# The order of expert weight loads and of TensorE's up steps in a hybrid decoder layer

## The reference

```python
logits = tok @ w_router + b_router
top_val, top_idx = lax.top_k(logits, 4)
top_w = softmax(top_val)
# for each expert e, on the rows of tokens that chose it:
hgu = tok[rows] @ w_gu[e] + b_gu[e]               # 1024 -> 2048
gate = minimum(hgu[:, 0::2], 7.0)
up = clip(hgu[:, 1::2], -7.0, 7.0)
act = (up + 1.0) * (gate * sigmoid(1.702 * gate))
y = act @ w_down[e] + b_down[e]                    # 1024 -> 1024
out = out.at[rows].add(y * wts)
```

## Time and profile before

| | |
|---|---|
| median of 3 runs | 1312.96 us (1312.86 to 1314.96) |
| profiled execution, its time | 1314.96 us |
| profiled execution, its span | 1313.1 us |
| TensorE busy | 86% of the span |
| TensorE granted clock, mean | 0.919 |
| moved by DMA | 455.49 MB, mean 347 GB/s |

### The profile page before, as it was taken

How to read it: one execution, slowest core, us unless ns; L and a number is a source line. 1 busy time by engine, 2 the same in 40 slices (tenths; PEclk the granted TensorE clock), 3 DMA queues, 4 the chain that set the end, 5 groups by cost and what they waited for, 6 DMA issues and landing times.

```text
span 1313.1 us, 19225 instructions
## 1 busy us (share of the span) xinstructions
PE 1127.0 (86%) x7477; PEld 535.2 (41%) x7478; DVE 270.2 (21%) x732; ACT 217.7 (17%) x486; POOL 17.9 (1%) x25
## 2 busy tenths in 40 slices
PE   8999999999989987659966966799697969799857
PEld 4564767888543333123322321233222323233311
DVE  3234424463141111001100100011101101111100
ACT  2115422353021101001100100111010101011101
POOL 1100101000000000000000000000000000000000
PEclk9999999999979999779987977899888979899978
DMA  9942337334559999999999999979999999999995
GB/s 338 344 140 94 113 136 263 130 132 184 201 207 422 425 426 426 426 427 426 423 426 425 428 426 427 426 301 422 424 426 427 422 426 425 427 426 427 426 427 223
DMA packets 66599, 455.49 MB, mean 347 GB/s; under 512 B 7524, under 2 KB 13384, under 8 KB 33800
## 3 DMA queue, kind: packets, MB, share of 16 engines
q1 hardware_dynamic: 66008, 454.20, 84.2%
q10 hardware_dynamic: 448, 0.60, 0.1%
q0 software_dynamic: 112, 0.26, 0.1%
HBM read 454.00 MB, written 1.05 MB: 347 GB/s over the span
## 4 chain that ended last, share of the span: by engine, by line
PE 64%; DMA 24%; SPq 8%; issue 2%; DVE 1%; ACT 1%; ACTq 0%; DVEq 0%
DMA mq<-in_b_gu 24%; PE bank L1060 17%; PE bank L1085 10%; PE bank L590 6%; PE bank L730 6%; SPq L394 4%; SPq L505 4%; PE bank L1020 4%; PE bank L1028 3%; PE bank L1039 3%; PE bank L639 2%; PE bank L926 2%; PE bank L892 2%; PE bank L579 1%; PE bank L616 1%
## 5 line engine op out<-in xcount | busy, mean ns | idle before, releaser
L1060 PE MATMUL bank<-mem 128*32 128x512 f32 x2944 | 360.4, 633 | 157.2 <-DMA mq<-in_b_gu 157.2
L1060 PEld LDWEIGHTS bank<-mem 128*32 128x32 f32 x2944 | 93.5, 114 | 369.5 <-issue 367.2
L1085 PE MATMUL bank<-mem 128*32 128x512 f32 x1472 | 177.1, 624 | 1.1 <-ACT mem L1376 1.1
L1821 DVE TENSOR_SCALAR mem<-bank 128x256 f32<-128x256 f32 x46 | 19.5, 425 | 748.8 <-PE bank L1060 748.8
L1382 ACT ACTIVATE mq<-bank 64x512 f32<-64x512 f32 x46 | 27.1, 590 | 468.9 <-PE bank L1085 468.9
L1085 PEld LDWEIGHTS bank<-mem 128*32 128x32 f32 x1472 | 44.7, 114 | 134.4 <-issue 133.7
L1020 PEld LDWEIGHTS bank<-mem,sc 128*128 128x128 f32 x736 | 85.6, 195 | 18.8 <-issue 18.8
L1020 PE MATMUL bank<-mem,sc 128*128 128x64 f32 x736 | 88.8, 280 | 0.3 <-DVE mem L1797 0.3
L1028 PE MATMUL bank<-mq,mem 128*128 128x512 f32 x184 | 85.1, 605 | 1.5 <-ACT mem L1399 1.5
L590 PE MATMUL bank<-mem 128*128 128x512 f32 x192 | 83.2, 592 | 0.0
L730 PE MATMUL bank<-mem 128*128 128x256 f32 x320 | 71.3, 381 | 0.0
(11 more groups left out here) (296 smaller groups left out, 787.6 us busy)
## 6 DMA issues: line engine op xcount, KB each, us to landing
mem<-in_w_gu SPq DMA_DIRECT2D x128, 2048.0 KB, 32.7
mem<-in_w_down SPq DMA_DIRECT2D x64, 2048.0 KB, 37.1
mem<-in_w_in SPq DMA_DIRECT2D x13, 2048.0 KB, 10.5
mem<-in_w_out SPq DMA_DIRECT2D x2, 2048.0 KB, 8.3
mem<-in_w_mem_kv SPq DMA_DIRECT2D x2, 1024.0 KB, 7.0
mem<-in_w_mem_kv SPq DMA_DIRECT2D x1, 2048.0 KB, 9.5
mem<-in_cmp_w_k SPq DMA_DIRECT2D x1, 2048.0 KB, 8.5
mem<-in_cmp_w_v SPq DMA_DIRECT2D x1, 2048.0 KB, 8.3
```

Of the source, the lines that this page charges most:

```text
L1060: mm = nc.tensor.matmul(BH[n][32 * s:32 * s + 32, :], xgT[:, k, 32 * n:32 * n + 32], w[:, c, 512 * s:512 * s + 512], start=k == 0, stop=k ...
L1085: mm = nc.tensor.matmul(BG[64 * hh + 32 * two:64 * hh + 32 * two + 32, :], actT[:, o:o + 32], w[:, 2 * c + two, 512 * hh:512 * hh + 512], ...
```

## The change

SyncE's list gets another order. In a round, the bias rows of seat n+1 come first, then its chunks 0 and 1, then chunks 4 and 5 (`w_down`) of seat **n** (`here`, into the slots that the last item `g` of seat n-2 leaves), then chunks 2 and 3 of seat n+1. A last round loads only `w_down` of seat 31. On TensorE, up1 moves ahead of `down` of the item before, behind up0 and bias, and `turn` moves between bias and up1.

```diff
--- before.py
+++ after.py
@@ -492,31 +492,40 @@
             sp.wait_ge(S("x2_ready"), 2)
             load_chunk(sp, 1, 4, True)
 
-            def load_round(n, odd, first=False):
-
-                f = sp.value_load(idx[0:1, bass.ds(n, 1)], min_val=0, max_val=ITEMS - 1)
-                ahead = sp.value_load(idx[0:1, bass.ds(n + (AT_ORDER + 1), 1)], min_val=0, max_val=NE - 1)
-                for q in range(4):
-                    sp.wait_ge(S("gu_done"), f * 4 + (q + 1))
-                    load_chunk(sp, ahead, q, not odd)
-                    if q == 1:
-                        sp.wait_ge(S("brow_used"), f + 1)
-                        for m in range(4):
-                            sp.dma_start(brow[not odd][32 * m:32 * m + 1, :],
-                                         b_gu[bass.ds(ahead, 1), 512 * m:512 * m + 512]).then_inc(brow_in[not odd], 16)
-                    if q == 1 and first:
-                        sp.wait_ge(S("bdn_done"), 1)
-                        load_chunk(sp, 1, 5, True)
-                for q in (4, 5):
-                    sp.wait_ge(S("down_done"), f * 2 + (q - 3))
-                    load_chunk(sp, ahead, q, not odd)
+            def load_round(n, odd, ups=True, downs=(4, 5)):
+
+                if ups:
+                    f = sp.value_load(idx[0:1, bass.ds(n, 1)], min_val=0, max_val=ITEMS - 1)
+                    ahead = sp.value_load(idx[0:1, bass.ds(n + (AT_ORDER + 1), 1)], min_val=0, max_val=NE - 1)
+                    sp.wait_ge(S("brow_used"), f + 1)
+                    for m in range(4):
+                        sp.dma_start(brow[not odd][32 * m:32 * m + 1, :],
+                                     b_gu[bass.ds(ahead, 1), 512 * m:512 * m + 512]).then_inc(brow_in[not odd], 16)
+                    for q in (0, 1):
+                        sp.wait_ge(S("gu_done"), f * 4 + (q + 1))
+                        load_chunk(sp, ahead, q, not odd)
+                if len(downs) == 2:
+                    here = sp.value_load(idx[0:1, bass.ds(n + AT_ORDER, 1)], min_val=0, max_val=NE - 1)
+                    g = sp.value_load(idx[0:1, bass.ds(n - 1, 1)], min_val=0, max_val=ITEMS - 1)
+                    for q in downs:
+                        sp.wait_ge(S("down_done"), g * 2 + (q - 3))
+                        load_chunk(sp, here, q, odd)
+                else:
+
+                    sp.wait_ge(S("bdn_done"), 1)
+                    load_chunk(sp, 1, 5, True)
+                if ups:
+                    for q in (2, 3):
+                        sp.wait_ge(S("gu_done"), f * 4 + (q + 1))
+                        load_chunk(sp, ahead, q, not odd)
 
             sp.wait_ge(S("idx_ready"), 1)
-            load_round(1, True, first=True)
+            load_round(1, True, downs=(5,))
             with sp.Fori(1, NE // 2 - 1) as r:
                 load_round(r * 2, False)
                 load_round(r * 2 + 1, True)
             load_round(NE - 2, False)
+            load_round(NE - 1, True, ups=False)
             for t in range(NT):
                 sp.wait_ge(S("out_left"), t + 1)
                 sp.dma_start(out_t[:, t, 0:512], x2[:, t, 0:512]).then_inc(S("out_done"), 16)
@@ -1105,22 +1114,25 @@
                 def left_early(odd):
                     up(0, left, 0, odd)
                     bias(0, odd)
+                    if not first:
+                        turn(i - 1, 1, j - 1)
+                    up(1, left, 0, odd)
 
                 def left_late(odd):
-                    for q in range(1, 4):
-                        up(q, left, 0, odd)
+                    up(2, left, 0, odd)
+                    up(3, left, 0, odd)
 
                 def right_early(odd):
                     up(0, right, 1, odd)
                     bias(1, odd)
+                    turn(i, 0, j)
+                    up(1, right, 1, odd)
 
                 def right_late(odd):
-                    for q in range(1, 4):
-                        up(q, right, 1, odd)
+                    up(2, right, 1, odd)
+                    up(3, right, 1, odd)
 
                 pe.wait_ge(S("g_evac"), j * 2 + 1)
-                if not first:
-                    turn(i - 1, 1, j - 1)
                 either(left, left_early)
                 pe.wait_ge(S("g_evac"), j * 2 + 2)
                 if not first:
@@ -1136,7 +1148,6 @@
                     pe.wait_ge(S("y_evac"), j * 2)
                     pe.wait_ge(S("st_evac"), j)
                     scatter()
-                turn(i, 0, j)
                 either(right, right_early)
                 pe.wait_ge(S("a_evac"), i + 1)
                 either(left, lambda odd: down(left, odd))
```

## The result

The changed kernel took 1341.45 us (median of 4 runs, 1340.57 to 1343.23) against 1313.76 us before in the same comparison; the ratio is 1.0222, 95% interval 1.0204 to 1.0240. It is slower, by 27.7 us. The prediction was 1333.6, with a range of 1322 to 1344: the time lies in the range, 7.9 us above the forecast. The profiled execution took 1341.32 us with a span of 1339.5, so the spans differ by 26.4 us and the forecast for that difference was 20.6.

The account below looks back on a forecast made before the run. The stream of weights was taken to pace the expert part. Start 2.6, seat 1 3.2, seat 8 7.1, seat 16 12.8 and end -5.1 sum to 20.6: span 1333.7, forecast 1333.6 us, range 1322 to 1344.

Parts of the forecast that it names:

- the end: Behind the last chunk: gu3(31) lands third from last, so the last seat finishes sooner; -5.1 us, bounds -7.3 and -0.8.
- seat 1: Near 421 us: stream runs dry at 420.3 waiting for item 2's bias, resumes 423.5; +3.2 us, bounds 2.3 and 3.9.
- stop at seat 8: New hole at a three-item seat: gu0 waits for the third item's bias; 7.1 us, bounds 5.1 and 9.1.
- stop at seat 16: Four-item seat: hole of 22.7 us in place of 9.9; +12.8 us, bounds 10.8 and 14.8.
- Depth of the queue: SyncE's list: dn(s+1) stands behind the wait for seat s's last item, leaving 6 chunks, 29.9 us, instead of 8, 39.9.
- Rivals A: Faster, 1298 us: bias rows and gu0 no longer wait for gu1, the hole at 871 closes; chance 0.06.
- B: Same, 1313.7 us: holes as before, start lost, tail won; chance 0.05.
- C: Slower, less, 1323.7 us: only two missing chunks at seat 16 count, seat 8 stays closed; chance 0.10.
- The 2.0 us for the clock: Added to the holes at seats 8 and 16: down behind short waits runs slower, 5.34 us instead of 3.64.
- Rival D: Slower, more, 1341.9 us: clock stays at 1.2 GHz beyond each wait, both holes at bound, slow scatter; chance 0.12.
- The restart: After a stop of the stream: 1.5 us from issue to flow; with the skill's 0.6 us, 2.7 less, estimate 1330.9.
- Order on TensorE: Same matmuls, nothing to win inside a busy stretch; with no stream to hide under, only turn's place counts, 0.7 us.

Follow-up runs that it names:

- one-item kernel: Kernel before with every expert cut to one item, tokens beyond the first 32 left out: 1310.69 us, before 1314.09.
- the two other edits: Changed kernel with w_down of seat n first and bias rows between chunks 0 and 1; with one transfer for the rows 1305.44 us, before 1313.01.

## Why the prediction was right, and where it was not

The stops, which are the mechanism, came as forecast. The total did not: of the 5.8 us by which the spans' difference was missed, 5.5 are one term, the end. It and seat 1 lie outside their own bounds, and that the sum up to the end of the bulk fits to 0.3 us is in part luck, as errors of -1.5, +0.7 and +1.6 cancel in part.

| term | forecast | measured | from |
|---|---|---|---|
| start | +2.6 | +2.5 | stream flows from 395.3 (157 GB/s in 394:396) against 392.8 |
| stop at seat 1 | +3.2 | +1.7 | window 420:430 |
| stop at seat 8 | +7.1 | +7.8 | windows 620:640 |
| stop at seat 16 | +12.8 | +14.4 | 24.3 against 9.9 |
| end of the bulk | +25.7 | +26.0 | 1321.0 (221 GB/s in 1320:1322) against 1295.0 |
| behind the bulk | -5.1 | +0.4 | 18.5 against 18.1 |
| span | +20.6 | +26.4 | |

**Depth of the queue: right.** The stops came where they were forecast and nowhere else, and moving two issues takes them away. Rivals A, B and C fall with the 24.3 us at seat 16 and the new stop at seat 8. The chain inside the stop is exact: from dn(16)'s second half at 866.56 to the end of the last item's bias at 894.10 are 27.5 us, and the prediction's steps give 31.8 - 19.9 + 15.6 = 27.5.

**The 2.0 us for the clock: right in size, wrong in cause.** TensorE ran the second half of `down` in 1.92 us, at full clock. What was late is dn(16) itself. By bytes the stream should run dry two chunks, 10.0 us, after it; it ran dry at 873.2 (254 GB/s in 872:874), 6.6 after: 3.4 us of slow landing. Of these about 2.1 come with the bias rows, since without them the distance was 8.7 (858.15 to 866.8). At seat 8 the excess of 2.7 us over the 5.1 without a clock term is of the same kind, but the bias rows are not its cause: dn(8) came about 7.5 us before the stream ran dry with them and without. There the last increment was 1.9 and 1.7 us behind, a lag that both kernels carry from the start of the expert part and that the stop at seat 8 wipes out; its cause stays open. Rival D, which put such an excess down to the clock, comes near the total (1341.9) with the wrong mechanism: its holes were to grow by the clock.

**Seat 1: too large by 1.5.** The item before was expected to take its old time; its up0 ran in 1.93 us instead of 3.21 (granted clock 1.00 in 400:410, 0.83 before; why is not shown), and gu0(3) was issued at 420.48, not 422.0.

**The restart.** From issue to flow it took 1.5 us in the kernel before and 1.3 here at seat 8 (635.49 to 636.8). By these rows the 0.6 us that the Trainium skill gives in "DMA: Bandwidth & Descriptors", "Specifications", as first-byte latency does not fit as the price of a restart; the estimate of 1330.9 that hung on it was further off.

**The end: the step that failed.** The prediction read "landed" from bytes: "gu3(31) is the third from last: landed 10.0 before the end T of the stream". It landed 4.5 before T (1316.5 against 1321.0), so TensorE's last `up`, activation and `down` lay about as late behind the bulk as in the kernel before, and most of `down` ran at the low clock (6.07 us; granted clock 0.50 in 1324:1328). The term was forecast at -5.1 and measured +0.4. The rows for this were there: 4.98 us a chunk by TensorE's waits, 4.92 by bytes. I took the one for pace and the other for flow and did not ask where 0.06 us a chunk go. They pile up as lag of one part of the stream, until a stop lets it catch up. At the end of the changed kernel the last increment of a chunk was 4.8 us behind the median, without bias rows 0.4: a difference of 4.4, as up3 started 4.5 and 8.8 us before T. By 0.06 us a chunk it should be 86 x 0.06 = 5.2, and 181 x 0.06 = 10.9 in the one-item kernel, where 9.9 was measured. The same lag explains the larger part of why closing the 9.9 us stop brought 3.4: the stop had set back 4.5 us of it (4.8 to 0.3), and the low clock in the last seat took 2.5 more.

**Order on TensorE: right** that it wins nothing by itself. That it would be worth 5.6 us together with the new list, by up1 ahead of the wait for `w_down`, is in no term of the prediction by itself; the chain of seat 16 has it in.

What stays open: which of the 16 parts lags, and why a row of 2 KB costs it some 0.1 us (4.9 us in 86 chunks with 57 rows). Leaving out 120 rows leaves out 240 packets, half of them under 512 B. The page's line on packets of the kernel before, and of the one without bias rows:

```profile
DMA packets 66599, 455.49 MB, mean 347 GB/s; under 512 B 7524, under 2 KB 13384, under 8 KB 33800
```

```profile
DMA packets 66359, 455.24 MB, mean 350 GB/s; under 512 B 7404, under 2 KB 13264, under 8 KB 33560
```

So each row is one packet of data and one small one, and does not spread over the engines. That it is the rows' own engine that lags is argued from the table of increments, the trickle of a sixteenth and the runs without rows; no row of the trace names the engine. One transfer of four rows has as many packets, and most of the lag is gone (1.9 us at the end in place of 5.2). The runs without rows also drop SyncE's wait for the bias and its issues, so their gain is not all lag.

## What to carry to other kernels

In a list that waits in order, a load belongs ahead of every wait that may be long, as soon as its own slot is surely free; sort by the longest time a slot can stay busy (here four items of 15.6 us on one seat), not by the usual one. Count the chunks behind the last issue and hold them against that time: that count gave each stop here to within 2 us. And when the pace read from waits differs from bytes over bandwidth by even 1%, look for what makes landings lag, since every chunk lands with its slowest piece (here up to 9.9 us behind the median one); in the kernel before, one transfer in place of four small ones was worth 5 us, and with the two other edits the kernel reached 1305.44 us against 1313.01.

## What the runs showed of the hardware

A 2 KB transfer into one partition, four for every 12.6 MB, slowed the landing of a full stream from 4.92 to 4.98 us a chunk while the bytes a second stayed at 426, and left up to ten microseconds of work at 25 to 41 GB/s behind the bulk. The last of a chunk's 16 increments fell behind their median by 0.06 us a chunk, to 5.2 us after 86 chunks and 9.9 after 181. One transfer of 4 x 2 KB in place of the four left 1.9 us, no rows 0.4. A stop of the stream sets the lag back (4.8 to 0.3 us), so closing a stop gives less than its windows show: 3.4 us for 9.9 here. Of the difference 2.5 us went to the low clock in the last seat, most of the rest to the lag.
